# One fused program of two transformer-like blocks: gate products spread among a scan's matmuls, router transposes and logits issued block by block, five instead of three sum products on TensorE, and unread matmuls behind three norms

## The reference, cut to what matters

```python
# first block
hx = modulate(rms_norm(x, norm1_g), sh1, sc1)
x_mix = token_mixer(hx @ w_in, ...)      # HGRN2 scan in chunks of 32, both directions, + Hyena branch
x = x + gt1 * x_mix                      # merged with sigmoid(g_a), sigmoid(g_b): 2048 gate logits a token
x = x + gt2 * hier_moe(modulate(rms_norm(x, norm2_g), sh2, sc2))   # 32 experts, top 2 of one group
x = rms_norm(x, final_norm_g)
# gla_chunk_scan, for each chunk of 32 tokens:
o = (q * exp(b)) @ S + masked_scores @ v
S = exp(total) * S + (k * exp(total - b)).T @ v
# router in hier_moe:
p_group = softmax(t @ wg + bg);  e_logits = t @ we + be
# second block, two layers
for layer in range(2):
    x = x + g1 * (hybrid_mixer(modulate(rmsnorm(x))) @ w_out)
    x = x + g2 * squared_relu_mlp(modulate(rmsnorm(x)), w_mlp1, w_mlp2)   # and ctx in layer 0
return rmsnorm(x, final_g)
```

## Time and profile before

| | |
|---|---|
| median of 3 runs | 1965.12 us |
| the runs | 1965.12, 1965.41, 1961.49 us |
| the profiled execution's own time | 1964.91 us |
| its span, first to last instruction | 1963.1 us |
| mean granted TensorE clock | 0.980 |
| PE busy | 1869.2 us (95%) |
| DVE, ACT, POOL busy | 817.9, 586.2, 389.0 us |

### The profile page before, as it was taken

The page is one execution under the profiler, slowest core; times in us unless marked ns, Lnnn a source line. Parts: engine busy times, 40 slices in busy tenths (PEclk is TensorE's granted clock), DMA queues, the critical chain, the costliest instruction groups (busy, mean ns, idle before and its releaser), DMA issues.

```text
span 1963.1 us, 26165 instructions
## 1 busy us (share of the span) xinstructions
PE 1869.2 (95%) x11248; PEld 1369.8 (70%) x11248; DVE 817.9 (42%) x1342; ACT 586.2 (30%) x892; POOL 389.0 (20%) x205
## 2 busy tenths in 40 slices
PE   6999999999999999989999899999999899889998
PEld 2777796964443443437887657888888688779998
DVE  2625245731111111116342844556555625574333
ACT  2523103331111111114112535222333411544554
POOL 2000000120000000006002032433343250025665
PEclk9999999989999999999999999999999899999999
DMA  9569817569999999992224004345444232414551
GB/s 358 181 241 363 313 44 278 204 264 428 427 427 427 428 426 427 427 413 94 86 86 141 23 33 171 140 166 188 150 150 152 92 122 87 174 53 163 175 198 37
DMA packets 111425, 429.84 MB, mean 219 GB/s; under 512 B 5706, under 2 KB 8821, under 8 KB 98512
## 3 DMA queue, kind: packets, MB, share of 16 engines
q1 hardware_dynamic: 109056, 416.56, 54.7%
q0 software_dynamic: 2256, 11.62, 1.6%
HBM read 427.11 MB, written 1.05 MB: 218 GB/s over the span
## 4 chain that ended last, share of the span: by engine, by line
PE 66%; DMA 16%; DVE 6%; PEld 5%; ACT 3%; issue 3%; PEldq 0%; POOL 0%; SPq 0%; POOLq 0%; DVEq 0%; ACTq 0%
PE bank L562 65%; DMA ring<-in_moe_w_down 7%; PEld bank L562 5%; DMA H<-in_moe_w_down 4%; DMA arena<-in_moe_w_down 4%; PE bank L577 1%; DVE H L1989 1%; DVE H_low L1996 1%; PEldq L541 0%; DMA ring<-in_w_in 0%; DMA arena<-in_hy_filt_w 0%; DVE arena L2514 0%; DVE ring_low L2590 0%; DVE ring_low L2171 0%; DVE ring_low L2584 0%
## 5 line engine op out<-in xcount | busy, mean ns | idle before, releaser
L562 PE MATMUL bank<-arena_r 128*128 128x256 f32 (+1 forms) x2176 | 592.0, 339 | 12.0 <-ACT arena_r L1386 6.5
L562 PE MATMUL bank<-arena_r,ring_low 128*128 128x512 f32 (+2 forms) x1920 | 596.5, 342 | 1.7 <-DVE H_low L1996 1.0
L562 PEld LDWEIGHTS bank<-arena_r 128*128 128x128 f32 x2176 | 385.1, 190 | 63.8 <-issue 15.9
L562 PE MATMUL bank<-arena 128*128 128x64 bf16 (+8 forms) x2892 | 366.7, 320 | 39.9 <-DMA arena<-in_hy_filt_w 11.5
L562 PEld LDWEIGHTS bank<-arena_r,ring_low 128*128 128x128 f32 (+1 forms) x1920 | 352.7, 188 | 47.6 <-issue 2.7
L562 PEld LDWEIGHTS bank<-arena 128*128 128x128 bf16 (+4 forms) x2892 | 207.5, 133 | 199.8 <-issue 170.7
L562 PE MATMUL bank<-H_low,arena_r 128*128 128x512 f32 (+1 forms) x672 | 217.1, 340 | 0.0
L562 PE MATMUL bank<-ring,arena 128*64 128x512 f32 x768 | 170.2, 599 | 8.5 <-DMA ring<-in_moe_w_down 8.5
L2572 DVE SCALAR_TENSOR_TENSOR X<-bank,mod,X 128x256 f32<-128x256 f32 x216 | 94.2, 478 | 196.6 <-PE bank L562 196.6
L1928 POOL TENSOR_TENSOR ring_low<-ring,arena_r 128x2048 fp32r<-128x2048 f32 x31 | 142.4, 4614 | 131.2 <-DVE ring_low L2584 68.8
L1400 ACT ACTIVATE arena<-bank 128x512 f32<-128x512 f32 (+2 forms) x106 | 51.2, 496 | 368.1 <-PE bank L562 367.9
(11 more groups left out here) (326 smaller groups left out, 1939.3 us busy)
## 6 DMA issues: line engine op xcount, KB each, us to landing
ring<-in_w_mlp SPq DMA_DIRECT2D x32, 2048.0 KB, 7.9
ring<-in_w_in SPq DMA_DIRECT2D x26, 2048.0 KB, 8.9
ring<-in_ada_w SPq DMA_DIRECT2D x24, 2048.0 KB, 12.2
ring<-in_moe_w_up SPq DMA_DIRECT2D x17, 2048.0 KB, 23.2
ring<-in_moe_w_gate SPq DMA_DIRECT2D x17, 2048.0 KB, 27.9
arena<-in_moe_w_up SPq DMA_DIRECT2D x15, 2048.0 KB, 22.5
ring<-in_moe_w_down SPq DMA_DIRECT2D x14, 2048.0 KB, 23.4
arena<-in_moe_w_down SPq DMA_DIRECT2D x13, 2048.0 KB, 23.5
```

Of the source, the lines that this page charges most:

```text
L562: ins = nc.tensor.matmul(o, l, r, start=start, stop=stop, skip_group_check=True)
```

## The change

- `sums`: for every norm but the first, POOL adds only blocks 1 to 3 (`blocks_added` is 4, in the first norm 6 as before), and TensorE makes five products: block 0, 4, 5, 6 and 7. `added_before` counts the additions of earlier norms.
- The scan: TensorE's wait for `masked` moves ahead of the first updates. `gate_products(m)` issues the next m of the same 32 gate products: 2 ahead of the waits for the turned keys and the context's state, 1 behind each group of 4 updates (8 in all), 3 behind each of the first six chunks' state products, 2 behind the last two.
- The router: per block k two transposes and two logit products; the logits of the two token blocks go to banks 4 and 5, DVE adds the bias in two operations, `logits` counts to 2, and ACT and DVE take the banks in the order 0, 2, 1, 3 (`TURNED`).
- `keep_busy(bank, n)`: n fp32 products of 128x512 that nobody reads, between TensorE's coming in at a phase end and its wait for the others: 5 in "merged", 8 in "l0_mlp", 5 in "l1_out".
- DVE: the low part of layer 1's second projection chunk is made before the norm, one half before l0_mlp's phase end, one behind it. In l1_out `low_w2` moves behind DVE's coming in at the phase end.

```diff
+        def blocks_added(call):
+
+            return KT - 2 if call == 0 else KT - 4
...
+            def keep_busy(bank, n):
+                for _ in range(n):
+                    mm(ps[bank], ident, base[:, 0:512])
...
-            def sums(call, nth, n, bank=6):
-
-                pe.wait_ge(S("squares_added"), 5 * nth)
-                for k in (0, KT - 2, KT - 1):
+            def sums(call, n, bank=6):
+
+                m = blocks_added(call)
+                pe.wait_ge(S("squares_added"), added_before(call) + m - 1)
+                for k in (0, *range(m, KT)):
...
+                gates = iter([(nt, k) for nt in range(4) for k in range(KT)])
+
+                def gate_products(m):
+                    for _ in range(m):
+                        nt, k = next(gates)
+                        gate_part(8 + d, nt, (k,))
+
                 chunk_in(win(8 + d))
+                pe.wait_ge(S("masked"), 2 * d + 2)
+                gate_products(2)
                 pe.wait_ge(S("turned_out"), 4 * d + 4)
                 pe.wait_ge(S("states_out"), 8 * d + 1)
...
                                inc="updates" if (j, h) == (3, 3) else None)
+                        gate_products(1)
                     if bi == 0:
-                        pe.wait_ge(S("masked"), 2 * d + 2)
...
-                        gate_part(8 + d, n // 2, range(4 * (n % 2), 4 * (n % 2) + 4))
+                        gate_products(3 if n < 6 else 2)
...
-            sums(1, 2, L)
-            phase_end(pe, "merged")
...
+            sums(1, L)
+            phase_end(pe, "merged", wait=False)
+            keep_busy(7, 5)
+            pe.wait_ge(S("phase"), 4 * (PHASES.index("merged") + 1))
+            pe.wait_ge(S("tables_in"), 64)
+            for k in range(KT):
+                pe.wait_ge(S("normed"), 16 + k + 1)
+                for tb in range(TB):
                     tr(ps[2 * tb + k // 4][:, (k % 4) * P:(k % 4 + 1) * P], H[:, k, tb * P:(tb + 1) * P], "tokens_passed" if k % 4 == 3 else None)
...
+                for tb in range(TB):
+                    mm(ps[4 + tb][:, 0:NR], H[:, k, tb * P:(tb + 1) * P], WR[:, k, :], k == 0, k == KT - 1, "logits" if k == KT - 1 else None)
...
+                phase_end(pe, f"l{l}_out", wait=False)
+                if l:
+                    keep_busy(7, 5)
+                pe.wait_ge(S("phase"), 4 * (PHASES.index(f"l{l}_out") + 1))
...
+                phase_end(pe, f"l{l}_mlp", wait=False)
+                if l == 0:
+                    keep_busy(0, 8)
+                pe.wait_ge(S("phase"), 4 * (PHASES.index(f"l{l}_mlp") + 1))
...
                 if l:
+                    next_low(1).then_inc(full[(L1 + 3) % RING], 16)
                     norm(ncall, 1 + l, 0, (0, 1))
...
+                phase_end(dve, f"l{l}_out", wait=False)
                 if l:
                     dve.wait_ge(S("w_high"), 24 + 3)
                     low_w2(MLP1 + 1, 0, 2048)
-                phase_end(dve, f"l{l}_out")
...
                     gains(2)
+                    next_low(0)
                     phase_end(dve, "l0_mlp")
```

More of the change, by code:

```diff
@@ L323, in expert @@
                 elif c == MRING - 1:
-                    sp.wait_ge(S("logits"), 1)
+                    sp.wait_ge(S("logits"), TB)
                 elif c >= MRING:
@@ L527, in build, with added_before @@
         W1h_cols, W2h_rows = W1h.rearrange("p (k n) -> p k n", k=KT), W2h.rearrange("p (k n) -> p k n", k=4)
+        def blocks_added(call):
+            return KT - 2 if call == 0 else KT - 4
+        def added_before(call):
+            earlier = {0: (), 1: (0,), 4: (0, 1), 5: (0, 1, 4), 6: (0, 1, 4, 5), 7: (0, 1, 4, 5, 6)}[call]
+            return sum(blocks_added(c) - 1 for c in earlier)
+        TURNED = (0, 2, 1, 3)
         AHEAD = 3
@@ L663, in _ @@
             ada_turn(1, 7, 1)
-            sums(0, 1, 2 * L, 1)
+            sums(0, 2 * L, 1)
             ada(2, 2, 6, blk=0)
@@ L1272, in _ @@
                         chunk_used()
-                sums(ncall, 3 + 2 * l, W)
+                sums(ncall, W)
                 ncall += 1
-                phase_end(pe, f"l{l}_out")
+                phase_end(pe, f"l{l}_out", wait=False)
+                if l:
+                    keep_busy(7, 5)
+                pe.wait_ge(S("phase"), 4 * (PHASES.index(f"l{l}_out") + 1))
                 def mlp_pair(i):
@@ L1347, in _ @@
                 flush()
-                sums(ncall, 4 + 2 * l, W)
+                sums(ncall, W)
                 ncall += 1
-                phase_end(pe, f"l{l}_mlp")
+                phase_end(pe, f"l{l}_mlp", wait=False)
+                if l == 0:
+                    keep_busy(0, 8)
+                pe.wait_ge(S("phase"), 4 * (PHASES.index(f"l{l}_mlp") + 1))
         @block.scalar
@@ L1553, in _ @@
             shifted(0, 1, (0,))
-            for b in range(4):
-                act.wait_ge(S("tokens_passed"), 2 + b + 1)
+            for i, b in enumerate(TURNED):
+                act.wait_ge(S("tokens_passed"), 2 + i + 1)
                 A_(by_blocks(HB[:, 0, b // 2, :], b % 2), ps[b][:, :].rearrange("t (p k) -> t k p", k=KT), ACT.Copy).then_inc(S("h_natural"), 1)
             for tb in range(TB):
-                act.wait_ge(S("h_rest"), 2 * tb + 2)
+                act.wait_ge(S("h_rest"), 3 + tb)
                 A_(HB[:, 1, tb, :], HN[:, tb, :], ACT.Copy).then_inc(S("h_natural"), 1)
@@ L1841, in add_squares @@
             def add_squares(call, n):
-                for k in range(1, KT - 2):
+                for k in range(1, blocks_added(call)):
                     pool.wait_ge(S("squares"), 8 * call + k + 1)
@@ L2232, in _ @@
             V.memset(CMB[:, :, NX:NX + 4], 0.0)
-            for b in range(4):
-                dve.wait_ge(S("h_natural"), b + 1)
+            for i, b in enumerate(TURNED):
+                dve.wait_ge(S("h_natural"), i + 1)
                 V.tensor_tensor(by_blocks(HN[:, b // 2, :], b % 2), ps[b][:, :].rearrange("t (p k) -> t k p", k=KT),
                                 by_blocks(HB[:, 0, b // 2, :], b % 2), ALU.subtract).then_inc(S("h_rest"), 1)
-            dve.wait_ge(S("logits"), 1)
-            link(V.tensor_tensor(LG, ps[4][:, 0:2 * NR].rearrange("p (a b) -> p a b", a=2),
-                                 bc(vec("rbias", 0, NR).unsqueeze(1), [P, TB, NR]), ALU.add))
+            for tb in range(TB):
+                dve.wait_ge(S("logits"), tb + 1)
+                i = V.tensor_tensor(LG[:, tb, :], ps[4 + tb][:, 0:NR], vec("rbias", 0, NR), ALU.add)
+            link(i)
             def r3(off, n):
@@ L2370, in _, with next_low @@
             dve.wait_ge(S("experts_done"), 1)
+            def next_low(a):
+                s = slice(2048 * a, 2048 * (a + 1))
+                dve.wait_ge(S("high_copied"), 12 + 2 + a + 1)
+                return V.tensor_tensor(low(L1 + 2)[:, s], slot(L1 + 2)[:, s], NEXTh[2 + a].bitcast(F32), ALU.subtract)
             def split_chunk(n, c=KT * 512):
@@ L2410, in _ @@
                 if l:
+                    next_low(1).then_inc(full[(L1 + 3) % RING], 16)
                     norm(ncall, 1 + l, 0, (0, 1))
                     ncall += 1
-                    n = L1 + 2
-                    for a in range(2):
-                        s = slice(2048 * a, 2048 * (a + 1))
-                        dve.wait_ge(S("high_copied"), 12 + 2 + a + 1)
-                        i = V.tensor_tensor(low(n)[:, s], slot(n)[:, s], NEXTh[2 + a].bitcast(F32), ALU.subtract)
-                    i.then_inc(full[(n + 1) % RING], 16)
                 for j in range(1 + l, 5):
@@ L2600, in _ @@
                     low_w2(MLP1 + 1, 0, 2048)
-                phase_end(dve, f"l{l}_out")
+                dve.wait_ge(S("phase"), 4 * (PHASES.index(f"l{l}_out") + 1))
                 norm(ncall, 1 + l, 1, (0, 1) if l == 0 else (0,))
```

9 lines of the change are left out of this document (removed).

## The result

The changed kernel takes **1987.2 us** in the median of four runs (1982.2 to 1993.5) against 1965.2 before: ratio 1.0105, 95% interval 1.0079 to 1.013. The forecast was 1962.5 with a range to 1968.0, so it is wrong in sign and size. The profiled execution took 1990.9 us (span 1989.1), 26.0 more than the one before.

The account below looks back on a forecast made before the run. TensorE was taken to bound the kernel (66% of the chain), except the expert stage, bound by loads. Scan -0.3, router -1.1, l0_out +1.6, l0_mlp -3.2, l1_out -0.2, l1_mlp +0.8 sum to -2.4: 1962.5 us, range 1957.0 to 1968.0.

Parts of the forecast that it names:

- Waits filled: Scan: two gate products go into TensorE's 0.88 us idle for the state's copy in each direction; -1.75 us.
- Broken runs: Scan: gate products between 32-row update groups lose their overlap and add switches, twelve places at 0.5; +6.0 us, bounds 0 to 8.8.
- Clock: Scan: gate products among the updates hold the clock up, removing three half-speed stretches of 3.4 us; -5.1 us.
- the clock keeps falling: Rival, scan: updates with products between stay too thin, the 5.1 us are not won; 1967.6 us, chance 0.17.
- low stretches in the scan: Sign: the prediction is wrong if clock stretches stay low in the scan.
- DVE in direction 1: Scan, direction 1: DVE needs 7.0 us to the last state, TensorE has 6.55 us of work; +0.5 us.
- Router: Router stage: logits finish earlier, but copies and a subtraction behind block 7 take back part; -1.1 us, bounds -3.0 to +0.7.
- my third rival: Rival, router: the clock holds through the stage, -3.0 us there; 1960.6 us, chance 0.12.
- l0_out: At l0_out: five 512-wide sums instead of three, with ACT, DVE and modulation waiting behind; +1.6 us.
- l0_mlp and layer 1's norm: Behind layer 0's MLP: sums and norm start earlier, eight unread products set TensorE's start; -3.2 us, bounds 0 and -6.
- l1_out: At l1_out: five unread products hold TensorE, +1.4, and the low clock stretch behind goes, -1.7; -0.2 us.
- l1_mlp: At l1_mlp: two more 256-wide products on the last path, less a little waiting; +0.8 us.

Follow-up runs that it names:

- `two_each`: The changed kernel with two gate products behind each 8 update records instead of one, fewer per chunk later; 1972.2 us, ratio 1.003.
- `scan_behind`: The changed kernel with four gate products behind each unbroken run of 32 update records, not one behind each 8; 1959.9 us, ratio 0.9971.
- `same_rows`: `scan_behind`'s order with all four groups of an unbroken run on rows 0 to 31 instead of four row positions; 1974.0 us, ratio 1.0046.
- `same_rows_twice`: `same_rows` with each run of 32 update records issued twice in a row; 1999.7 us, ratio 1.018.
- `doubled`: `scan_behind`'s order with each run of 32 update records issued twice in a row; 1970.5 us, ratio 1.0024.
- `full_rows`: The changed kernel with each scan update record summing over all 128 rows instead of its group's 32; 1962.3 us, ratio 0.9975.

## Why the prediction was wrong

The forecast was -2.4, the two profiles show +26.0. The step that failed is the clock term of the scan, forecast -5.1 and found at +12.2; two others were too small or of the wrong sign (broken runs +9.2 for +6.0, router +4.0 for -1.1).

- **Waits filled, -1.75.** Right. The old order at full clock is 73.1 less three half-clock stretches (5.1), 68.0; the unbroken new order at full clock takes 66.5, so -1.5.
- **Broken runs, +6.0.** The mechanism was right, the size too small: 12 places at 0.77 are +9.2, a little over my upper bound of 8.8. The lost overlap was 0.34 (I took 0.3), the turn 0.37 to 0.43 (I took 0.2, since no gap shows in the rows). The row with 0.33 idle ahead of a run was the better guide. What the prediction cites from the Trainium skill, TensorEngine Tiling (Array Packing), Tiling Modes, that a change of the tiling mode drains TensorE, fits this price; that the time is such a drain, no run shows.
- **Clock, -5.1.** This is the step that failed: "if the gate products among the updates hold the clock up". The scan has 93.0 - 66.5 - 9.2 = 17.3 us more than the broken order would need at full clock; before, it was 5.1. So the term was +12.2, not -5.1. Half of the 37.5 us at half clock is 18.7, which checks the 17.3 from the other side. I had read the earlier trace rows as "busy, and still it falls", and concluded that more work in between must help. What the rows held was how thin that work is: of the 39 records in those 3.4 us, 32 stand on 32 rows and six have only 32 columns. Breaking the run takes away its overlap and stretches the thin part from 2.7 to 6.8 us. The rival "the clock keeps falling" named the place but priced it as a gain not made (1967.6), with no case in which the change itself adds low stretches. That it can get worse had to be an end of the range. The prediction's last paragraph did name low stretches in the scan as a sign of being wrong, and that sign came.
- **DVE in direction 1, +0.5.** Not seen: in the changed scan TensorE waits for DVE only once, 0.5 us, ahead of the score products.
- The sum is -1.5 + 9.2 + 12.2 = 19.9. It meets the two profiles by its making, since the clock's term is what the other two leave; the 18.7 above and the 9.0 of `two_each` are the checks on its parts.
- **Router, -1.1; measured +4.0** (+3.4 in the mean of the nine profiles against the one of before, +2.7 against the mean of the three with the old order). The logits came earlier, as in my third rival, and the clock held until behind them. I wrote that "two copies and a subtraction" follow and did not list POOL's subtractions among the moved work, nor ask what runs on DVE at that time. The Trainium skill, SBUF — State Buffer, "SBUF: two separate sides", says that DVE and GpSimd share one pair of ports as an exclusive lock, which a DVE operation with two SBUF inputs needs only against a GpSimd one that reads SBUF. The rows agree: 2.05 us for an operation of 0.17, ending with POOL's. Of the trace before, I could have had the price of the overlap: 2.13 us for each POOL row.
- **l0_out, +1.6.** Measured +1.5.
- **l0_mlp and layer 1's norm, -3.2.** The second chunk starts 23.6 us behind the MLP's end instead of 26.3: -2.7. To l1_out's sums it is -2.0 here and in `scan_behind`, whose profiles have low stretches of 6.8 and 10.2 us there, and -4.0 to -5.3 in the nine other profiles with this part unchanged. That the unread products set the start was right (1572.8 to 1579.9, when DVE's first block had been ready from 1577.5). DVE's second low part waited for TensorE's end of phase until 1572.83, which I had not listed; it cost nothing that shows.

```profile
1567.98 4.71 PE L572 MATMUL bank<-H,base 128*128 128x512 f32 x10
1572.79 7.13 PE L572 MATMUL bank<-base 128*128 128x512 f32 x16
...
1591.53 0.47 PE L572 MATMUL bank<-arena_r 128*128 128x512 f32 x1 [0.21 <-ACT arena L1427]
```

- **l1_out, -0.2; l1_mlp, +0.8.** Measured +0.3 and +0.8.

What stays open: why the changed order keeps the clock low for 34 to 37.5 us of the scan while `two_each` has 1.8 of it, and 5.0 behind. Between the two stand one more product per place and the same turns. That thin, unoverlapped work alone brings the clock down is shown; how much the turns add to it in the broken run is not.

## What to carry to other kernels

Don't put full-height work between matmuls on different 32-row groups: it cost 0.77 us a place inside a run here, and with single products the clock on top; put it ahead of or behind the whole run. A forecast that rests on the clock needs both signs in its range, since the edit that is to hold it up changes what TensorE does in the stretches that decide. When a step gets ready later, list what the other engines start on it, and look whether POOL then reads SBUF beside a chain of small DVE operations.

## What was not expected of the hardware

- TensorE's clock fell to half in stretches in which the profile shows it busy all of the time, and which began when its work stood on one group of 32 rows: 23.8 and 47.8 us low in the scan of `same_rows` and `same_rows_twice`. Twice the 32-row records on four row positions gave 6.8 (`doubled`), four times the rows in every record gave none (`full_rows`).
- 32 records on one row position took 3.74 us, on four 2.72: overlap gives a factor of 1.4 for fp32 records of 128 columns.
- A turn between 32-row and full-height work cost 0.37 to 0.43 us for going in and out, worked out from `full_rows` and `same_rows`, though PE's row shows no gap.
- Two DVE operations on 128x4 and 128x8 elements took 2.1 us each beside POOL's subtraction, and 0.17 without it.
- With 13.7 us of half clock in the router stage instead of 3.4, the stage took only 1.5 us more. The unread products that held the clock up had started the transposes 2.2 us later.
